# Hybrid decoder layer on one core: order and layout of the last norm, the last transposes and the output stores

## What is computed

```
x = x + concat(GroupRMSNorm(y_A), GroupRMSNorm(y_B)) @ w_out
h = RMSNorm(x)
x = x + (silu(causal_dwconv3(h @ w_gate)) * (h @ w_up)) @ w_down
y_prompt = rmsnorm(xp, final_norm_g)          # xp: 512 x 2048
y_sample = rmsnorm(xs, final_norm_g)          # xs:  64 x 2048

def rmsnorm(x, g):
    xf = x * rsqrt(mean(x * x, axis=-1) + EPS)
    return xf * g
```

## Time and profile before

| | |
|---|---|
| median of 3 runs | 2306.56 us (2304.87 to 2307.8) |
| the profiled execution | 2307.53 us |
| its span | 2305.9 us |
| busy on PE | 2265.4 us (98%) |
| busy on DVE, ACT, POOL | 1655.2, 1014.6, 504.1 us |
| mean granted TensorE clock | 0.993 |

### The profile page before, as it was taken

The page is one execution under the profiler, slowest core; times in us unless marked ns, Lnnn a source line. Parts: engine busy times, 40 slices in busy tenths (PEclk is TensorE's granted clock), DMA queues, the critical chain, the costliest instruction groups (busy, mean ns, idle before and its releaser), DMA issues. The chain is left out here.

```text
span 2305.9 us, 44056 instructions
## 1 busy us (share of the span) xinstructions
PE 2265.4 (98%) x16978; PEld 2253.8 (98%) x16978; DVE 1655.2 (72%) x2237; ACT 1014.6 (44%) x1599; POOL 504.1 (22%) x599
## 2 busy tenths in 40 slices
PE   7999999999999999999999999999999999999996
PEld 7999999999999999999999999999999999999996
DVE  6347754545422676888888888888888798888885
ACT  6224321213211353444454444545444565555575
POOL 2310000000222101111111111111112356655574
PEclk9999999999999999999999999999999999999998
DMA  7322232223533244453444435344446566775432
GB/s 243 98 76 71 75 90 76 83 80 85 183 117 94 73 142 121 128 165 119 152 134 140 150 119 165 123 146 138 136 157 214 179 230 217 235 231 200 173 93 101
DMA packets 369228, 320.15 MB, mean 139 GB/s; under 512 B 8680, under 2 KB 348771, under 8 KB 363616
## 3 DMA queue, kind: packets, MB, share of 16 engines
q1 hardware_dynamic: 346464, 203.98, 30.2%
q0 software_dynamic: 22656, 114.69, 13.4%
HBM read 258.32 MB, written 60.31 MB: 138 GB/s over the span
## 5 line engine op out<-in xcount | busy, mean ns | idle before, releaser
L1892 PE MATMUL ps<-h_hi,w_hi 128*128 128x288 f32 x1728 | 513.1, 297 | 0.0
L1894 PE MATMUL ps<-h_hi,w_lo 128*128 128x288 f32 x1728 | 509.3, 295 | 0.0
L1893 PE MATMUL ps<-h_lo,w_hi 128*128 128x288 f32 x1728 | 509.2, 295 | 0.0
L2251 PE MATMUL ps<-form,dw_hi 128*128 128x288 f32 x1232 | 365.9, 297 | 3.7 <-DVE dw_lo L1790 2.6
L2252 PE MATMUL ps<-form,dw_hi 128*128 128x288 f32 x1232 | 362.6, 294 | 0.0
L2253 PE MATMUL ps<-form,dw_lo 128*128 128x288 f32 x1232 | 362.0, 294 | 0.0
L1892 PEld LDWEIGHTS ps<-h_hi,w_hi 128*128 128x128 f32 x1728 | 324.7, 188 | 0.8
L1893 PEld LDWEIGHTS ps<-h_lo,w_hi 128*128 128x128 f32 x1728 | 324.7, 188 | 0.1
L1894 PEld LDWEIGHTS ps<-h_hi,w_lo 128*128 128x128 f32 x1728 | 324.5, 188 | 0.0
L1288 DVE TENSOR_TENSOR w_lo<-raw,w_hi 128x1024 fp32r<-128x1024 f32 x128 | 163.0, 1302 | 198.4 <-ACT w_hi L799 198.1
L1790 DVE TENSOR_TENSOR dw_lo<-down,dw_hi 128x512 fp32r<-128x512 f32 (+1 forms) x282 | 242.5, 866 | 73.6 <-ACT dw_hi L813 73.0
(11 more groups left out here) (298 smaller groups left out, 5258.2 us busy)
## 6 DMA issues: line engine op xcount, KB each, us to landing
raw<-in_w_gate_dram SPq DMA_DIRECT2D x88, 512.0 KB, 4.3
raw<-in_w_in_dram SPq DMA_DIRECT2D x80, 512.0 KB, 4.3
down<-in_w_down_dram SPq DMA_DIRECT2D x32, 1024.0 KB, 5.4
form<-act_scratch POOLq DMA_DIRECT2D x28, 1152.0 KB, 6.8
act_scratch<-stage POOLq DMA_DIRECT2D x46, 576.0 KB, 4.4
raw_c<-in_w_up_dram SPq DMA_DIRECT2D x40, 512.0 KB, 3.8
raw_d<-in_w_up_dram SPq DMA_DIRECT2D x40, 512.0 KB, 5.0
raw<-in_w_out_dram SPq DMA_DIRECT2D x32, 512.0 KB, 3.9
```

The lines of the kernel that those rows point to most:

```text
L1892: te.matmul(out, whi, xhi, start=start, stop=False)
L1893: te.matmul(out, whi, xlo, start=False, stop=False)
L1894: return te.matmul(out, wlo, xhi, start=False, stop=stop)
L2251: te.matmul(out, dw_hi[:, m % 4, j, :], act_f[:, j, 0, :], start=start and j == 0, stop=False, skip_group_check=True)
```

## The change

It has five parts, all about the final norm:
- Sums first. PE sums `facc` over the partitions before the transposes of tile 15 and not after them. There are now six sums, since the 64 sample rows are summed twice: once for partitions 0 to 63, once (with tokens 448 to 575) so that they come out on partitions 64 to 127. They go to PSUM bank 0 (prompt) and bank 1 (samples), and are signalled apart.
- Square root's table. One square root on an unused column of `small` is put into visit 3 (`elif v == 3`). The table that square roots need is loaded there, and the load at the end is gone.
- Left halves first. Columns 0 to 1023 of all blocks need only tiles 0 to 7, but the scaling needs the sums of all tiles. Both engines now begin with left halves; DVE copies tile 15 out of PSUM after it has scaled the left half of block 0, in two quarters.
- Samples on 128 partitions. Tiles 8 to 15 of the samples are transposed as 128-column blocks (tokens 448 to 575), so that the sample rows come out on partitions 64 to 127. `out_nat[0:64, 4, 0:1024]` holds their left half and `out_nat[64:128, 4, 0:1024]` their right half; one DVE operation of 128 x 1024 scales both.
- Stores. SP stores what DVE scaled (`OUT_D`: five pieces, among them the samples' left half from partitions 0 to 63), POOL stores what ACT scaled (`OUT_A`: five pieces), and after its second the samples' right half from partitions 64 to 127. All pieces have 1024 columns but the first two, of 512.

```
--- before.py
+++ after.py
@@ -395,6 +395,10 @@
             a, c, d = ((0, 2, 3), (2, 3, 0), (3, 0, 2))[(v - LAST_V) % 3]
             return a, 1, c, d
 
+        LOW, HIGH = slice(0, AW), slice(AW, DM)
+        OUT_D = ((0, slice(0, AW // 2)), (0, slice(AW // 2, AW)), (0, HIGH), (TB, LOW), (2, HIGH))
+        OUT_A = ((1, LOW), (2, LOW), (3, LOW), (1, HIGH), (3, HIGH))
+
         block = ctx.enter_context(nc.Block())
 
 
@@ -491,17 +495,18 @@
                              w_down[0][2 * f0 * P:2 * (f0 + n) * P, g * 2 * P:(g + 1) * 2 * P].rearrange(
                                  "(k p) c -> p k c", p=P)).then_inc(down_landed[v % 2], 16)
 
-            for n in range(2):
-                sp.wait_ge(out_a, n + 1)
-                cols = slice(n * AW, (n + 1) * AW)
-                sp.dma_start(y_prompt[0][P:2 * P, cols], out_nat[:, 1, cols]).then_inc(stored_sp, 16)
-            sp.wait_ge(out_a, 3)
-            sp.dma_start(y_prompt[0][3 * P:4 * P, :], out_nat[:, 3, :]).then_inc(stored_sp, 16)
+            samples = y_sample.rearrange("b s d -> (b s) d")
+            for n, (tb, cols) in enumerate(OUT_D):
+                sp.wait_ge(out_d, n + 1)
+                if tb < TB:
+                    sp.dma_start(y_prompt[0][tb * P:(tb + 1) * P, cols], out_nat[:, tb, cols]).then_inc(stored_sp, 16)
+                else:
+                    sp.dma_start(samples[:, 0:AW], out_nat[0:SAMP, TB, 0:AW]).then_inc(stored_sp, 16)
             sp.wait_ge(rows_out, 5 * 16)
             sp.wait_ge(v_out[0], 16 * HEADS // 2)
             sp.wait_ge(v_out[1], 16 * HEADS // 2)
-            sp.wait_ge(stored_sp, 3 * 16)
-            sp.wait_ge(stored, 4 * 16)
+            sp.wait_ge(stored_sp, 16 * len(OUT_D))
+            sp.wait_ge(stored, 16 * (len(OUT_A) + 1))
 
 
         @block.gpsimd
@@ -775,14 +780,12 @@
                             pool.wait_ge(down_landed[(v + 2) % 2], 16 * ((v + 2) // 2 + 1))
                         load_form(NQ * (ch + 1) + t, piece_done, D0 + NQ * v + t - 4)
             fin_sum(KT - 2)
-            for n in range(2):
-                pool.wait_ge(out_d, n + 1)
-                cols = slice(n * AW, (n + 1) * AW)
-                g.dma_start(y_prompt[0][0:P, cols], out_nat[:, 0, cols]).then_inc(stored, 16)
-            pool.wait_ge(out_d, 3)
-            g.dma_start(y_sample.rearrange("b s d -> (b s) d"), out_nat[0:SAMP, TB, :]).then_inc(stored, 16)
-            pool.wait_ge(out_d, 4)
-            g.dma_start(y_prompt[0][2 * P:3 * P, :], out_nat[:, 2, :]).then_inc(stored, 16)
+            for n, (tb, cols) in enumerate(OUT_A):
+                pool.wait_ge(out_a, n + 1)
+                g.dma_start(y_prompt[0][tb * P:(tb + 1) * P, cols], out_nat[:, tb, cols]).then_inc(stored, 16)
+                if n == 1:
+                    pool.wait_ge(out_d, 4)
+                    g.dma_start(y_sample.rearrange("b s d -> (b s) d")[:, AW:DM], out_nat[SAMP:P, TB, 0:AW]).then_inc(stored, 16)
 
 
         @block.scalar
@@ -1252,6 +1255,8 @@
                 bank_snap(v, 2, 3, bank_a, u2_snap)
                 if v == 2:
                     rows_stage()
+                elif v == 3:
+                    a.activation(small[:, 17:18], eps_t, ACT.Sqrt)
                 if v in LATE_ROUNDS:
                     act_hi(PAIRS - 1, LATE_ROUNDS[v])
                 more = v + 1 < VISITS * len(CHUNKS)
@@ -1265,12 +1270,17 @@
                     last_tile(2 * gv, 3 * v + 2)
             last_tile(KT - 1, 3 * VISITS * len(CHUNKS))
             act.wait_ge(fssq_done, 1)
-            a.activation(rms_nat[:, 0:TB], ps[:, 0, 0:TB], ACT.Sqrt, bias=eps_t, scale=1.0 / DM)
-            a.activation(rms_nat[0:SAMP, TB:TB + 1], ps[0:SAMP, 0, TB:TB + 1], ACT.Sqrt, bias=eps_t[0:SAMP],
-                         scale=1.0 / DM).then_inc(frms_ready, 1)
+            a.activation(rms_nat[:, 0:TB], ps[:, 0, 0:TB], ACT.Sqrt, bias=eps_t, scale=1.0 / DM).then_inc(frms_ready, 1)
+            act.wait_ge(fssq_done, 2)
+            for rows, c in ((slice(0, SAMP), TB), (slice(SAMP, P), TB + 1)):
+                a.activation(rms_nat[rows, TB:TB + 1], ps[rows, 1, c:c + 1], ACT.Sqrt, bias=eps_t[rows],
+                             scale=1.0 / DM).then_inc(frms_ready, 1)
             act.wait_ge(frrms_ready, 1)
-            act.wait_ge(f_ready, KT)
-            for tb, cols in ((1, slice(0, AW)), (1, slice(AW, DM)), (3, slice(0, DM))):
+            for n, (tb, cols) in enumerate(OUT_A):
+                if n == 0:
+                    act.wait_ge(f_ready, KT // 2)
+                elif n == 3:
+                    act.wait_ge(f_ready, KT)
                 a.activation(out_nat[:, tb, cols], out_nat[:, tb, cols], ACT.Copy,
                              scale=rms_nat[:, tb:tb + 1]).then_inc(out_a, 1)
 
@@ -1837,7 +1847,9 @@
                 dve.wait_ge(f_t, j + 1)
                 v.tensor_copy(out_nat[:, 0:TB, j * P:(j + 1) * P],
                               ps[:, 4 + 2 * s, :].rearrange("p (b c) -> p b c", b=TB))
-                v.tensor_copy(out_nat[0:SAMP, TB, j * P:(j + 1) * P], ps[0:SAMP, 5 + 2 * s, 0:P]).then_inc(f_ready, 1)
+                rows = slice(0, SAMP) if j < KT // 2 else slice(SAMP, P)
+                c = j % (KT // 2) * P
+                v.tensor_copy(out_nat[rows, TB, c:c + P], ps[rows, 5 + 2 * s, 0:P]).then_inc(f_ready, 1)
 
             NV = VISITS * len(CHUNKS)
             for vi in range(NV):
@@ -1867,19 +1879,24 @@
                     if LATE_ROUNDS[vi] == 1:
                         act_t4(PAIRS - 1)
             add_a(NV - 1, KT - 2)
-            out_store(14, 0)
             dve.wait_ge(fsq_ready, KT)
             dve.wait_ge(facc_done, KT)
             v.tensor_tensor(facc[:, :], facc[:, :], fin_sq[(KT - 1) % 2][:, :], ALU.add).then_inc(facc_done, 1)
-            out_store(15, 1)
+            out_store(14, 0)
             dve.wait_ge(frms_ready, 1)
-            v.reciprocal(rms_nat[:, 0:TB], rms_nat[:, 0:TB])
-            v.reciprocal(rms_nat[0:SAMP, TB:TB + 1], rms_nat[0:SAMP, TB:TB + 1]).then_inc(frrms_ready, 1)
+            v.reciprocal(rms_nat[:, 0:TB], rms_nat[:, 0:TB]).then_inc(frrms_ready, 1)
             dve.wait_ge(frrms_ready, 1)
-            dve.wait_ge(f_ready, KT)
-            for tb, cols in ((0, slice(0, AW)), (0, slice(AW, DM)), (TB, slice(0, DM)), (2, slice(0, DM))):
-                n = P if tb < TB else SAMP
-                v.tensor_scalar(out_nat[0:n, tb, cols], out_nat[0:n, tb, cols], rms_nat[0:n, tb:tb + 1], None,
+            for n, (tb, cols) in enumerate(OUT_D):
+                if n == 0:
+                    dve.wait_ge(f_ready, KT // 2)
+                elif n == 2:
+                    out_store(15, 1)
+                    dve.wait_ge(f_ready, KT)
+                elif n == 3:
+                    dve.wait_ge(frms_ready, 3)
+                    v.reciprocal(rms_nat[:, TB:TB + 1], rms_nat[:, TB:TB + 1]).then_inc(frrms_ready, 1)
+                    dve.wait_ge(frrms_ready, 2)
+                v.tensor_scalar(out_nat[:, tb, cols], out_nat[:, tb, cols], rms_nat[:, tb:tb + 1], None,
                                 ALU.mult).then_inc(out_d, 1)
 
 
@@ -2263,7 +2280,10 @@
                     pe.wait_ge(bank_read, 3 * LAST_V)
                 for b in range(TB):
                     te.transpose(ps[:, 4 + 2 * s, b * P:(b + 1) * P], fin_g[s][:, b * P:(b + 1) * P], ident[:, :])
-                te.transpose(ps[0:SAMP, 5 + 2 * s, 0:P], fin_g[s][:, SEQ:T], ident[:, :]).then_inc(f_t, 1)
+                if j < KT // 2:
+                    te.transpose(ps[0:SAMP, 5 + 2 * s, 0:P], fin_g[s][:, SEQ:T], ident[:, :]).then_inc(f_t, 1)
+                else:
+                    te.transpose(ps[:, 5 + 2 * s, 0:P], fin_g[s][:, T - P:T], ident[:, :]).then_inc(f_t, 1)
 
             for vi in range(VISITS * len(CHUNKS)):
                 ba, bb, bc, bd = banks(vi)
@@ -2298,12 +2318,15 @@
                 pe.wait_ge(u2_snap, vi + 1)
                 down_product(vi, 6, ba, False, True)
             out_t(14)
+
+            pe.wait_ge(facc_done, KT + 1)
+            pe.wait_ge(d_read, VISITS * len(CHUNKS))
+            pe.wait_ge(bank_read, 3 * VISITS * len(CHUNKS) - 1)
+            for c, t0, n in [(tb, tb * P, P) for tb in range(TB)] + [(TB, SEQ, SAMP), (TB + 1, T - P, P)]:
+                mm = te.matmul(ps[0:n, 0 if c < TB else 1, c:c + 1], facc[:, t0:t0 + n], ones[:, 0:1], start=True, stop=True)
+                if c in (TB - 1, TB + 1):
+                    mm.then_inc(fssq_done, 1)
             out_t(15)
-            pe.wait_ge(facc_done, KT + 1)
-            for tb in range(TB + 1):
-                n = P if tb < TB else SAMP
-                last = te.matmul(ps[0:n, 0, tb:tb + 1], facc[:, tb * P:tb * P + n], ones[:, 0:1], start=True, stop=True)
-            last.then_inc(fssq_done, 1)
 
 
 # ---- launch: one core; inputs and outputs as the reference has them ----
```

## The result

The changed kernel takes 2310.41 us (median of 22 runs, 2306.9 to 2315.35), the kernel before 2306.84 us (22 runs beside it, 2303.61 to 2312.84). The ratio over all runs is 1.0013, with a 95% interval of 1.0008 to 1.0019: **3.0 us slower** (1.8 to 4.4). The two medians lie a little further apart, 3.57 us; this text goes by the ratio and its interval, here and for the experiments. That is within 0.2%, but on the other side of no change than forecast, and outside the predicted range. The profiled execution took 2311.59 us, its span is 2310.0 us.

The account below looks back on a forecast made before the run. PE was taken to bound the kernel (98% busy), with only the end, bound by stores, able to shorten. Earlier data -1.55, supply +0.35 and packets -0.1 gave -1.3 us, so 2305.3 us, range 2302.7 to 2307.6.

Parts of the forecast that it names:

- The transposes with 128 sample columns in place of 64, one a tile, are priced at 0 too: PE's wider sample transposes, one a tile, were to cost 0; taken whole, the excess is 0.5 us.
- Over 0.2% slower would need a fault that no row suggests: Whole kernel: a slowdown of more than 0.2% was given a chance of 0.04.
- rival (c): First two stores: a 2 KB packet takes as long as a 4 KB one; +0.9 us, 2307.4 us, chance 0.08.
- First data: Tail: sums, scaling and first store come sooner, so output data begin to move 1.55 us earlier.
- Supply: Stores after the first two quarters: a gap before the next pieces loses 0.35 us, between 0 and 0.65.
- Packets: Output stores: packet time over 16 engines 12.7 us, 0.1 less than before, bounds 12.2 and 13.2.
- Rival (a): Sample stores stay slow: 128 packets at 0.30 us, 0.5 us more; -0.8 us, 2305.8 us, chance 0.24.
- Rival (b): Sample stores: the two halves overlap entirely; -1.8 us, 2304.7 us, chance 0.12.
- End: SP's last wait, for the other engines after the landings, stays 3.3 us whatever is stored.
- Rival (d): SP's 3.3 us end wait is POOL clearing its queue and shrinks; -4.6 us, 2302.0 us, chance 0.06.
- (e): Early start of left-half scaling doesn't happen, waiting for something later; +0.3 us at most, 2306.9 us, chance 0.04.
- Sum: Tail terms together: -1.55 + 0.35 - 0.1 = -1.3 us, bounds -2.15 and -0.5.

Follow-up runs that it names:

- wide_transpose: Kernel before with only the 128-column sample transposes for tiles 8 to 15, copies still from rows 0 to 63: last chunk 96.58 us, ratio 0.9995.
- delay_probe: Kernel before with two small copies on partitions 0 to 63 ahead of the sample copy of tiles 8 to 15: last chunk 96.75 us, ratio 1.0002.
- spread_alone: Kernel before with only the samples put on 128 partitions and stored by POOL as two halves: last chunk 99.49 us, ratio 1.0017.
- drain_probe: Kernel before, DVE waiting for its own sample copy of tiles 8 to 13 before going on: last chunk 99.11 us, ratio 1.0018.
- no_spread: Changed kernel with the samples back on partitions 0 to 63, stored as one piece by SP: last chunk 96.75 us, ratio 1.0002.
- late_table: Changed kernel without the square root in visit 3, so the table loads at the end: last chunk 99.44 us, ratio 1.0012.
- swap_after: Changed kernel with each tile's sample copy ahead of the prompt's copy: last chunk 99.22 us, ratio 1.0013.
- full_copy: Changed kernel, sample copies of tiles 8 to 15 on all 128 partitions from partition 0, one more scaling: last chunk 98.63 us, ratio 1.0005.
- pool_waits: Changed kernel, POOL waiting for one more DVE rest before its second-half addition in visits 44 to 47: last chunk 99.02 us, ratio 1.0008.
- short_delay: Kernel before with one small copy (64 x 36, partitions 0 to 63) ahead of the sample copy of tiles 8 to 15: last chunk 96.73 us, ratio 0.9998.
- swap_128: Kernel before, sample copy of tiles 8 to 15 128 partitions high and ahead of the prompt's copy: last chunk 98.63 us, ratio 1.0009.

## Why the prediction was wrong

**The step that failed** is the one that priced the spread outside the tail: "The transposes with 128 sample columns in place of 64, one a tile, are priced at 0 too". For the transposes that holds (wide_transpose). But the part has a second instruction, DVE's copy onto partitions 64 to 127, and it was given no price and no cover was named. Its own 0.2 us a tile would still have been hidden (delay_probe). What it cost is 2.78 us in visits 46 and 47 (13.07 and 14.09 us for 12.25 and 12.12), by PE's waits for DVE, of which this chunk had none before. A sign of it stands in the trace before all the same: POOL's addition takes 2.49 us in visit 45 and 0.81 us in the same trace at 2248.63, so DVE and POOL contend there, and it is POOL that loses. "Over 0.2% slower would need a fault that no row suggests" rested on the same omission; no rival named this place. The slower rival (c) was another mechanism, and it was wrong.

**The tail** was right in kind, too large in size. By terms, against the profiled execution before:

- First data: predicted 1.55 us earlier, measured 7.11 - 5.70 = 1.41 us earlier, counted from the last product. Scaling starts 2290.03 - 2287.62 = 2.41 us behind the start of the last addition; the steps gave 2285.58 - 2283.3 = 2.28.
- Supply: predicted 0.35 us lost. Data took 14.58 us from first to last with 13.11 us of packets, 1.47 us idle; before 13.47 with 12.96, 0.51 idle. So **1.0 us lost, not 0.35**. 0.6 of it is the hole before 2293.4. Two steps were mis-sized. POOL's store was given "SP's 0.85 us" from issue to data; it took 2292.05 to 2293.4, 1.35 us. And its issue was forecast 5.95 us after the last product and came 6.34 us after it, as PE's six sums and the sample roots behind them ended later (ACT scales from 4.89 us after the last product, forecast 4.53). Most of the rest lies in the last microsecond, where the queues run out less evenly (share 0.15, before 0.36); where the slow sample packets run, the DMA engines are not idle. The full gap of 0.65 us was nearer for the hole. The prediction took it from what the Trainium skill says of GpSimd's descriptors (SBUF — State Buffer, "SBUF: two separate sides"); the issue took 0.81 us beside DVE's scaling and 0.53 to 0.58 us later without it, which agrees, but no run separates the cause.
- Packets: predicted 12.7 us, 0.1 less; measured 13.11 against 12.96, 0.15 more. Rival (a) was right: the samples' packets stay slow, 0.36 us for 4 KB in the window above. Rival (b) is out. (c) is out too: 2 KB take 0.087 us.
- End: 3.3 us, as before. Rival (d) is out, and (e) as well, since the sums wait for DVE's addition alone.
- Sum: -1.41 + 0.96 + 0.15 = -0.3 us, where -1.3 was forecast. One tail may be off by some tenths: eight kernels with the old end (all but spread_alone and drain_probe, which have 25.7 and 25.9) range from 24.4 to 25.3 us, mean 24.9; with the new end the changed kernel, no_spread, late_table and swap_after have 24.05 to 24.5, mean 24.3, and full_copy and pool_waits, with work or waits of their own, 25.2 and 25.5. By the means of the first two groups the new end gives 0.6 us.
- Clock: a term that the prediction did not have, and a good part of that scatter. With the old end the root starts 4.38 us after the last product where the clock falls later than that (before, short_delay, swap_128), and up to 5.02 us after it where the clock falls during the sums (delay_probe, at 3.4 us: the same 10 passes take 1.79 us for 1.16). With the new end the sums are over sooner, and the root starts 3.80 to 3.81 us after the last product in all these kernels but late_table. So some of the 0.6 us is that the sums more often escape the slower clock.

Together +2.78 - 0.25 = +2.5 us by the profiles, +3.0 (1.8 to 4.4) by the runs.
